# Context and latents as two streams of one unrolled program

## What is computed

```python
sh1, sc1, g1, sh2, sc2, g2 = _modulation(cond, w_mod[l], b_mod[l])
h = _rmsnorm(x, norm1[l]) * (1 + sc1) + sh1
mix, s_f, s_b = _token_mixer(h, ...)       # 4 heads of gated linear attention, Fourier mixing, gates, w_out
x = x + g1 * mix
h = _rmsnorm(x, norm2[l]) * (1 + sc2) + sh2
x = x + g2 * _peer(h, w_query[l], sub_keys[l], expert_u[l], expert_v[l])
```

```python
a = jax.nn.gelu(jnp.einsum('nd,nhkd->nhk', xb, expert_u[ib]))
coef = wb * a
return jnp.einsum('nhk,nhkd->nd', coef, expert_v[ib])
```

## Time and profile before

| | us |
|---|---|
| runs (median; lowest to highest of 3) | 5711.72; 5695.85 to 5712.79 |
| profiled execution, its own time | 5713.33 |
| its span | 5711.7 |
| mean granted TensorE clock | 0.894 |
| busy: TensorE / DVE / POOL / ACT | 4505.0 / 2640.2 / 2457.6 / 1032.5 |
| DMA: moved, mean | 1513.50 MB, 265 GB/s |
| of it the gathers (q0) / the weights (q1) | 1347.03 MB / 162.02 MB |

### The profile page before, as it was taken

One profiled execution on the slowest core, in us unless ns is written; L12 is line 12 of the kernel. 1 busy time (PEld: TensorE's weight loads), 2 busy tenths in 40 slices (PEclk: granted clock), 3 DMA queues, 4 the chain that ended last, 5 costly groups with the idle time before them and its releaser, 6 DMA issues.

```text
span 5711.7 us, 47022 instructions
## 1 busy us (share of the span) xinstructions
PE 4505.0 (79%) x14627; PEld 2413.8 (42%) x14627; DVE 2640.2 (46%) x6085; ACT 1032.5 (18%) x2332; POOL 2457.6 (43%) x2629
## 2 busy tenths in 40 slices
PE   7998996997777677767789989969967677767676
PEld 3565895443332232232335559944323232323223
DVE  1233334555556555554313323255555555555643
ACT  1232331111111111111102224311111111111111
POOL 0000002666666666666500000036666666666663
PEclk9999998998888888888889999989988888888888
DMA  6210225999999999999851112279989999999996
GB/s 204 65 44 19 71 76 179 368 370 340 367 353 365 359 365 362 359 365 363 331 186 45 43 32 64 72 253 364 364 334 360 368 365 361 368 359 365 360 363 249
DMA packets 575500, 1513.50 MB, mean 265 GB/s; under 512 B 45704, under 2 KB 244864, under 8 KB 574912
## 3 DMA queue, kind: packets, MB, share of 16 engines
q0 software_dynamic: 371264, 1347.03, 62.1%
q1 hardware_dynamic: 201728, 162.02, 9.4%
q10 hardware_dynamic: 2304, 2.10, 0.1%
HBM read 1506.24 MB, written 4.72 MB: 265 GB/s over the span
## 4 chain that ended last, share of the span: by engine, by line
PE 53%; issue 17%; POOL 10%; DMA 9%; DVE 5%; another core or an unknown queue 3%; ACT 2%; DVEq 1%; ACTq 0%; POOLq 0%; SPq 0%
PE pair L498 51%; POOL ubuf L478 5%; POOL vbuf L484 5%; DMA ubuf<-in_expert_u,idx 4%; DMA vbuf<-in_expert_v,idx 4%; DVE ubuf L1421 1%; ACT diag L863 1%; PE pair L654 1%; PE pair L659 1%; DMA slot<-in_w_mod 1%; DVE hist L1211 1%; DVEq L1214 0%; DMA slot<-in_w_query 0%; DVE hT L1081 0%
## 5 line engine op out<-in xcount | busy, mean ns | idle before, releaser
L498 PE MATMUL pair<-vbuf,diag 128*128 128x512 f32 x5120 | 2558.1, 658 | 975.0 <-issue 575.5
L1421 DVE CUSTOM_DVE_ANT_0 ubuf<-pair,ubuf 128x1024 f32<-128x1024 f32 x1280 | 1555.1, 1222 | 1415.4 <-DMA ubuf<-in_expert_u,idx 1185.0
L498 PEld LDWEIGHTS pair<-vbuf,diag 128*128 128x128 f32 x5120 | 1054.4, 212 | 2453.7 <-issue 2275.5
L484 POOL DMA_INDIRECT vbuf<-in_expert_v,idx x1280 | 1211.0, 946 | 930.0 <-PE pair L498 389.0
L478 POOL DMA_INDIRECT ubuf<-in_expert_u,idx x1280 | 1208.0, 944 | 454.3 <-issue 370.4
L498 PE MATMUL pair<-hT,slot 128*128 128x512 f32 (+1 forms) x2304 | 641.5, 438 | 19.7 <-DVE hT L1090 19.7
L863 ACT ACTIVATE diag<-cst,coef 128x128 f32<-128x128 f32 x1280 | 391.3, 388 | 887.3 <-issue 517.6
L498 PEld LDWEIGHTS pair<-hT,slot 128*128 128x128 f32 x2304 | 357.2, 194 | 301.9 <-issue 278.1
L471 POOL DMA_DIRECT2D skey<-in_sub_keys x16 | 11.4, 715 | 927.9 <-DVE xT L1297 839.9
L863 ACT ACTIVATE gel<-araw 128x8 f32<-128x8 f32 x160 | 33.3, 208 | 1911.9 <-issue 978.2
L498 PE MATMUL pair<-slot,scond 128*2 128x256 f32 x768 | 191.2, 408 | 35.7 <-DMA slot<-in_w_mod 29.8
(11 more groups left out here) (210 smaller groups left out, 3420.5 us busy)
## 6 DMA issues: line engine op xcount, KB each, us to landing
slot<-in_w_mod SPq DMA_DIRECT2D x48, 1024.0 KB, 11.5
slot<-in_w_query SPq DMA_DIRECT2D x32, 1024.0 KB
ubuf<-in_expert_u,idx POOLq DMA_INDIRECT x1280
vbuf<-in_expert_v,idx POOLq DMA_INDIRECT x1280
slot<-in_w_in SPq DMA_DIRECT2D x16, 1024.0 KB, 5.3
wraw<-in_w_in SPq DMA_DIRECT2D x32, 512.0 KB, 3.9
slot<-in_w_in SPq DMA_DIRECT2D x24, 512.0 KB, 4.6
wraw<-in_w_gla_out SPq DMA_DIRECT2D x16, 512.0 KB
```

The costliest lines, as they stand in the source:

```text
L484: pool.indirect_dma_start(vbuf[at % V_RING][:, :], None, v_rows, bass.IndirectOffsetOnAxis(ap=idx[:, at // PICKS, at % PICKS:at % PICKS + ...
L498: return pe.matmul(out, lhsT, rhs, start=first, stop=last)
L1421: v.tensor_tensor_reduce(ubuf[at % U_RING][:, :], pair[0][:, :], ubuf[at % U_RING][:, :], 1.0, 0.0, ALU.mult, ALU.add, araw[n % 2][:, j:j ...
```

## The change

The loop over the layers is gone; both layers are written out. Each layer is cut into four programs: the mixer of the context, the mixer of the latents, the expert layer of the context, that of the latents. Every step of a program carries a planned time in microseconds, and `weave` writes the steps of two or three programs into each engine's stream in the order of these times. The context's experts stand among the latents' mixer of the same layer, and the latents' experts among the context's mixer and the modulation of the next layer. A plan only sets an order; at run time each engine waits for its semaphores as before.

- All weights come through one ring of four slots of 1 MB in the order `FILLS`. The mixer's weights (33.7 MB) are loaded once for each stream, so twice a layer; `w_query` was so before.
- The rings are per stream: context u 4 and v 4, v eight places behind u; latents u 6 and v 4, v four places behind u. A group is four places.
- The context's v rows are added on DVE into `acc` in SBUF (one product-and-add of 128 x 1024 a place, a drain before it), without diagonals and TensorE. The latents' stay on TensorE.
- The dots read the tokens from SBUF (`hT` in place, or `xnat0` for the first tile of the latents), since the mixer needs the PSUM.
- The latents' queries and scores of all eight heads come ahead of the latents' gathers on TensorE; the first choice waits for those of heads 0 to 3, the first addition for all.

```diff
-GS = 8
...
-U_RING, V_RING = 8, 8
...
+GS = 4
+U_RING, V_RING = (4, 6), (4, 4)
+LAG = 2 * GS
...
-SLOTS = 6
...
+SLOTS = 4
...
+def weave(*programs):
...
+    while waiting:
+        first = min(waiting, key=lambda w: w[:2])
+        waiting.remove(first)
+        at = next(first[2], None)
+        if at is not None:
+            waiting.append((max(at, first[0]), first[1], first[2]))
...
+CTX_PLACE, CTX_AT, CTX_CHOOSE = 3.4, 195.0, 60.0
+LAT_PLACE, LAT_AT, LAT_CHOOSE = 2.6, 125.0, 88.0
...
+                p_end, lag = NT[s] * PICKS, (LAG, GS)[s]
+                ring_u, ring_v, index = U_RING[s], V_RING[s], peer[s].idx
+                for p in range(p_end + lag):
+                    if p < p_end:
...
+                        if p >= ring_u:
+                            hold(pool, s_dot, place_of(l, s) + p - ring_u + 1)
+                        pool.indirect_dma_start(peer[s].u[n % ring_u][:, :], None, u_rows, bass.IndirectOffsetOnAxis(
...
+                    p -= lag
+                    if p >= 0:
+                        n = ring_no(l, s, p)
+                        if p >= ring_v:
+                            hold(pool, s_pv[s], n - ring_v + 1)
+                        pool.indirect_dma_start(peer[s].v[n % ring_v][:, :], None, v_rows, bass.IndirectOffsetOnAxis(
...
-                        v.tensor_tensor_reduce(ubuf[at % U_RING][:, :], pair[0][:, :], ubuf[at % U_RING][:, :],
-                                               1.0, 0.0, ALU.mult, ALU.add, araw[n % 2][:, j:j + 1]).then_inc(s_dot, 1)
-                        if j == 1 and n >= 1:
-                            coefficients(n - 1)
...
+                v.tensor_tensor_reduce(rows_of, x, rows_of, 1.0, 0.0, ALU.mult, ALU.add,
+                                       araw[n % 3][:, p % GS:p % GS + 1]).then_inc(s_dot, 1)
...
+                            last = stt(acc[:, :], row, coef[n % 3][:, j:j + 1], acc[:, :], ALU.mult, ALU.add)
+                        last.then_inc(s_pv[s], 1)
...
+                    dot(l, s, p, xnat0[:, :, :] if t == 0 else natural(s, t))
+                    n = p // GS
+                    if p % GS == 1 and n >= 1:
+                        coefficients(l, s, n - 1).then_inc(s_coef, 1)
...
+            weave(mix(0, CTX, clock(0.0, 0.5)), modulation(0, clock(0.0, 0.5)))
+            weave(mix(0, LAT, clock(85.0, 1.0)), context_peer(0))
+            weave(latent_peer(0), mix(1, CTX, clock(310.0, 1.6)), modulation(1, clock(310.0, 1.6)))
+            weave(mix(1, LAT, clock(85.0, 1.0)), context_peer(1))
+            weave(latent_peer(1), last_norm(CTX, clock(200.0, 1.5)))
+            weave(last_norm(LAT, clock(0.0, 1.0)))
```

More of the change, by code:

```diff
@@ L284, in build @@
+    s_at = [area[LAT].end]
+    xin = place("xin", [P, T // P, D], at=s_at)
+    rows0 = place("rows0", [24, P], at=s_at)
+    rows = [place(f"rows{l}", [80, P], at=s_at) for l in range(DEPTH)]
     ident = cst[:, C_ID:C_ID + 128]
@@ L751, in context_queries @@
[L751 to L759 removed]
+                yield at(NORM2_US)
@@ new lines, in latent_peer @@
+                groups = NT[s] * PICKS // GS
+                per_tile = PICKS // GS
+                out_pending = None
+                for n in range(groups):
+                    yield lat_added(n)
+                    t = n // per_tile
+                    if n == 0:
+                        pe.wait_ge(s_sc, 2 * (n0 + PH))
+                    if n % per_tile == 0 and t >= 1:
+                        pe.wait_ge(s_on2, tile_no(l, s, t))
+                    pe.wait_ge(s_diag, l * groups + n + 1)
@@ L971, in _ @@
-                act.wait_ge(s_f2, l + 1 + START)
+                    if s == LAT and h < HEADS - 1:
+                        hold(act, s_om, om_no(l, s, h) + OM[s])
+                        states(h + 1)
+                    if h < HEADS - 1:
+                        yield at(x0 + 87.0)
+                        copy_query(it + 1)
+                f0, nb = f1_no(l, s), len(b.all)
+                yield at(FOURIER_US + 1.0)
+                for i in range(2 * nt):
+                    act.wait_ge(s_f1, f0 + i + 1)
+                    af(a.ab[:, i // 2, 2 * (i % 2):2 * (i % 2) + 2, :, :], b.all[i % nb], ACT.Copy).then_inc(s_f1c, 1)
@@ new lines, in natural, with update @@
+            def natural(s, t):
+                at = COLS[s].start + t * P
+                return hT[:, :, at:at + P]
+            def update(l, s, t, half):
+                dve.wait_ge(s_ot[s], 2 * tile_no(l, s, t) + half + 1)
+                at = slice(COLS[s].start + t * P, COLS[s].start + (t + 1) * P)
+                for k in range(4 * half, 4 * half + 4):
+                    last = stt(xT[:, k, at], ps[0][:, (k % 4) * P:(k % 4 + 1) * P], modT[l][:, 40 + k, s:s + 1], xT[:, k, at],
+                               ALU.mult, ALU.add)
+                    if t == NT[s] - 1 and k < 4 * half + 3:
+                        last.then_inc(s_x2[s], 1)
+                last.then_inc(s_xu[s], 1)
+                if t == NT[s] - 1:
+                    dve.drain()
+                    dve.sem_inc(s_x2[s], 1)
@@ new lines, in context_peer @@
+            def context_peer(l):
+                s = CTX
+                for u in range(2):
+                    yield from choose(l, s, u, clock(CTX_CHOOSE + 63.0 * u, 3.0))
+                for p in range(PICKS + LAG):
+                    yield ctx_place(p)
+                    if p == 0:
+                        dve.wait_ge(s_xnc, l * (NT[0] + NT[1]) + 1)
+                    if p < PICKS:
+                        dot(l, s, p, natural(s, 0))
+                    q = p - LAG
+                    if q >= 0:
+                        n, j, r = q // GS, q % GS, ring_no(l, s, q)
+                        if j == 0:
+                            coefficients(l, s, n)
+                        dve.drain()
+                        dve.wait_ge(s_gv[s][r % V_RING[s]], gathered(V_RING[s], r))
+                        row = peer[s].v[r % V_RING[s]][:, :]
+                        if q == 0:
+                            last = ts(acc[:, :], row, coef[n % 3][:, j:j + 1], None, ALU.mult)
+                        else:
+                            last = stt(acc[:, :], row, coef[n % 3][:, j:j + 1], acc[:, :], ALU.mult, ALU.add)
+                        last.then_inc(s_pv[s], 1)
+                for half in range(2):
+                    yield ctx_place(PICKS + LAG) + 6.0 + 4.0 * half
+                    update(l, s, 0, half)
```

2217 lines of the change are left out of this document (1231 added, 986 removed).

## The result

| | before | after |
|---|---|---|
| runs on one chip, median (lowest to highest of 4), us | 5703.78 (5691.39 to 5712.79) | 5892.33 (5879.7 to 5902.21) |
| ratio of the times, 95% interval | | 1.033 [1.030, 1.036] |
| span of the profiled execution, us | 5711.7 | 5893.6 |
| mean granted TensorE clock | 0.894 | 0.847 |
| busy TensorE / DVE / POOL / ACT, us | 4505.0 / 2640.2 / 2457.6 / 1032.5 | 4464.8 / 3048.5 / 2807.6 / 1393.3 |

A forecast was written before the change was run, and what follows sets the result against it. Bound: memory, less what a short ring costs. 404 + 760 + 135 + 1690 + 14 + 760 + 135 + 1536 + 54 = 5488, say 5490 us; forecast 5300 to 5690 (0.54), wider range 5040 to 5800.

The forecast's parts named there:

- the turn of the ring: Latent gathers: POOL-to-POOL cycle for four places, 10.8 us or 12.6 with TensorE cold; 3.0 us a place taken, bounds 2.6 to 3.4.
- the row of 3.77: Profile row of before: after 3.04 us idle, TensorE's four addition records took 3.77 us, nearly all at half clock.
- wrong as a whole if the latent pace is above 3.3: Sign for the latent gathers: a pace above 3.3 us a place would refute the forecast, which took 3.0.
- The context under layer 0's gathers: Layer 1's context work under layer 0's latent gathers: charged 154 us, bounds 0 and 320, making those gathers 1690.
- Mixers, queries and tail: Terms: context mixer to 404 us, latent mixers 760 a layer, bare latent queries 135 a layer, end 54.
- the split into 578, 70 and 110: Latent mixer with context gathers: 578 us mixer, 70 norms and queries ahead, 110 in-order waits; 758, say 760, a layer.
- the rival of a cover without gain: Latent mixer: each context place costs it the DMA wait, 760 becomes 900 twice, 5770 us in all; chance 0.13.
- a warm TensorE: Rival for the latent gathers: TensorE keeps its clock or turns overlap, 2.6 us a place, 5080 in all; chance 0.17.
- memory, less what a short ring costs: Bound of the kernel before's gathers: DMA at 2.56 us a place, raised to 2.926 by POOL waiting for v buffers.
- the floors of 2.56 and 2.49: Gathers: least time a place, 2.56 us for DMA at 411 GB/s and 2.49 for POOL's two issues.
- The port rival: Each DMA issue waits out a dot with two SBUF operands: 3.69 us a place, 6200 in all; chance 0.09.
- The clock rival: TensorE at half clock throughout the latent gathers: 3.45 us a place, about 6000 in all; chance 0.07.

The follow-up runs named there:

- e10: Changed kernel with coefficients formed one dot earlier and latents' rings of u 5 and v 5 instead of 6 and 4: 5348.78 us, ratio 0.9385.
- e7: Kernel before with the coefficients of a group formed one dot earlier: 5716.29 us, ratio 0.997.
- e9: Kernel before with v rows of 2 KB instead of 4 KB, gathers and additions as many: 5697.96 us, beside 5711.0 for before.
- e5: e1 with the dots of tiles 1 to 3 in layer 1 reading their tokens from PSUM: 5452.74 us, ratio 0.951.
- e1: Changed kernel with the latents' coefficients formed one dot earlier: 5454.07 us, ratio to before 0.951.
- e4: Changed kernel with four idle matmuls of 512 columns behind each group of additions in layer 1: 5796.07 us.
- e13: Kernel before with v gathers of 64 rows instead of 128 and additions over 64 rows: 6408.92 us.
- e14: e10 with the latents' v gathers of 64 rows instead of 128 and additions over 64 rows: 6081.25 us.
- e15: Kernel before with v gathers fetching 64 rows while additions stay 128 rows high: 6156.11 us.

## Why the prediction was wrong

**The step that failed** is the turn of the ring in the latent gathers. The mechanism was named (POOL, fetch, dot, coefficients, diagonals, cold TensorE, back to POOL); its size was not. The means over all groups of layer 1, from the single records of the trace:

| leg of a turn | forecast, us | measured, us |
|---|---|---|
| v issue to u issue | 1.24 | 1.50 |
| u issue to its dot | 4.5 | 5.36 |
| dot to coefficients made | 1.51 | 1.31 |
| diagonals, and TensorE's start | 1.5 | 1.36 |
| TensorE's first place, to POOL's next v | 2.04, cold 3.84 | 4.44 |
| sum | 10.8, cold 12.6 | 13.97 |

Three sizes were too small. *The fetch* was read from the first gather of a layer, with no gather ahead of it; under load it takes 0.86 more. *The cold addition*: the row of 3.77 was at hand (the granted clock was 0.50 in those 3.77 us), but 12.0 was taken, between the two ends, though the change makes most bursts cold ones; the measured first place of 3.62 on average is near that row, and the release took 0.82 more, not 0.3. The recorded cold sum is itself 0.2 short: 3.77 in place of 1.74 makes 12.8 of the 10.8, not 12.6. *The issue* lost 0.26 to the port and to small waits. Two legs in the middle were too large, by 0.34 together. From 12.0 to 14.0 is 2 us a group, and 256 groups make about 500 us: 0.5 a place. The measured legs add up to the pace, 13.97 / 4 = 3.49, so these errors go into the time in full. The range had 3.4 a place as its edge; 3.51 and 3.62 lie beyond, and "wrong as a whole if the latent pace is above 3.3" is what came.

**The context under layer 0's gathers** was charged 154 us and cost 55: 1853 against 1798 with none. That the turn's gaps took it in is argued from e10, where the ring is loose and it costs 1613 - 1489 = 124. By luck this error hid 99 us of the other.

**The rest of the sum held.** Mixers, queries and tail came within 15 us each; the mixer with the context's gathers took 762 and 760 for 760 (the split into 578, 70 and 110 wasn't measured), so the rival of a cover without gain, 900, is out. So is that of a warm TensorE: the granted clock of layer 1's latent gathers was 0.81. Taking the context's places off the gather stretch is a real gain: with the ring loosened the changed kernel is at 0.951 and 0.9385. The change as made loses because it also shortens the rings.

**The bound of before was misread.** The earlier trace rows show POOL idle for 3.86 us ahead of a v gather, with TensorE named. The single records say that the additions which that gather needed had ended by 2011.11, and POOL's wait ended at 2017.09. Of the 148 pauses of over 1 us ahead of a v gather in before only 21 ended within 0.5 us of the addition needed. Beyond the usual 0.30 these pauses sum to 536 us, 0.42 for each of the 1280 places: that is the way from POOL's floor of 2.49 to 2.91, nearly the whole of it.

TensorE is named rightly all the same, and this is the main thing that the earlier trace rows hide. 136 of the 148 pauses ended within 0.1 us of a recorded update of the very semaphore that the additions raise, but the update came late: 126 waits ended more than 1 us after the addition, at the median 8.1 us after, and 92 of the updates that ended a wait have at least two others within 0.3 us, where additions are 1.7 us apart. The ends of matmuls in a profile are modelled, but in after 995 of the 998 updates recorded during the gathers came within 0.02 us of such an end. So POOL stood for word of additions long done. What holds the updates back, no run shows.

e7 agrees: there the additions come earlier, and it gains 0.3%. So "memory, less what a short ring costs" was wrong in both halves (e7, e9), and the floors of 2.56 and 2.49 are not reached by any kernel here; 2.9 is. Why word comes late, so that POOL pauses some 4 us, at the median every 20 gathers, isn't settled: e7 speaks against the turn, e5 against the dots' operands, e9 against the bytes, and whether it is the number of rows or of gathers no run told. A v ring of more than eight buffers in before, in which POOL could run on over a late update, was not tried.

**The port rival.** The Trainium skill (SBUF — State Buffer, Who interferes with whom) says that a DVE instruction with two SBUF inputs contends with a GpSimd instruction that reads SBUF, since its second input comes through a read interface that the two share. The prediction set that aside by the earlier trace rows, where an issue ended before a product did. It looked at the wrong product. Two pairs in the timeline of e1:

```profile
4607.31 1.22 DVE L1711 CUSTOM_DVE_ANT_0 ubuf_lat<-hT,ubuf_lat 128x1024 f32<-128x1024 f32 x1 [1.62 <-DMA ubuf_lat<-in_expert_u,idx_lat]
4608.03 1.31 POOL L635 DMA_INDIRECT vbuf_lat<-in_expert_v,idx_lat  x1 [0.30 <-issue]
...
4610.36 1.23 DVE L1711 CUSTOM_DVE_ANT_0 ubuf_lat<-hT,ubuf_lat 128x1024 f32<-128x1024 f32 x1 [1.82 <-DMA ubuf_lat<-in_expert_u,idx_lat]
4610.89 1.50 POOL L635 DMA_INDIRECT vbuf_lat<-in_expert_v,idx_lat  x1 [0.31 <-PE pair L656]
```

The dots end at 4608.53 and 4611.59; the issues that began under them end at 4609.34 and 4612.39, 0.81 and 0.80 after. In the earlier trace rows the issue at 2009.00 ends at 2010.22, 0.81 after the product that began at 2008.18. An issue that starts first isn't lengthened: 742 issues of e1 under which a dot began took 0.94 at the median. So the trace agrees with the rule, and its mechanism was wrongly set aside; but the mean issue of after is 1.07 to 1.13 (its four groups of gathers), far from the 1.35 at which the port would have decided, and in e5 taking it away changed nothing.

**The clock rival** gave 3.45 a place for TensorE at half clock throughout. After ran at a granted clock of 0.81 to 0.86 in its latent gathers, so this wasn't its case (e4: 0.9 of 14 us); e13 ran into it for another reason, at just that pace.

## What to carry to other kernels

When a change shortens a ring, write out the turn leg by leg and take every leg from a row under load and in the clock state that the shorter ring itself makes; then compare turn over group size with the pace of before, and where the two are close, loosen the ring (one step earlier for the last consumer, one buffer moved) before anything else is judged. A releaser in a profile is an inference: before a pause is called a ring wait, see whether it ended with the very instruction that frees that buffer, or with a late update of its semaphore, which an earlier instruction would not mend. A gain on one stage and a loss in another came in one change here, and only undoing one part at a time showed that the idea was worth 5 to 6%.

## What the runs showed of the hardware

- TensorE busy for 0.97 to 0.99 of a window with additions over 64 rows was granted 0.53 and 0.50 (e13, e14), that is nearly all or all of it at 1.2 GHz of its 2.4; additions over 128 rows, busy 0.71 in e13's stretch of before, had 0.85.
- A gather into partitions 0 to 63 beside gathers into all 128 takes DMA to a share of 1.02 at 250 GB/s (e15), against 1.03 at 411 GB/s. The Trainium skill (SBUF — State Buffer, Door 1: The DMA port swizzle) states that partitions 0 to 63 reach only half of the DMA ports, the even ones. By an estimate from that page the even ports have as much to write for a place as in before, so a place would take as long as there; the measured one takes longer (633 issues in 1000 us against 688), so the trace agrees in that the smaller gathers saved nothing, and shows a slowing beyond it.
- An issue of a gather that begins under a dot with two SBUF operands ends 0.81 us after the dot (median of 852 in e1); without one it takes 0.94.
- The semaphore updates of TensorE's additions can reach a waiting POOL late: in before 307 of the 918 recorded during the gathers came more than 1 us after the last addition that had ended; in after, at 570 gathers in 1000 us instead of 684, none of the 998 came so late.
